# Two weight splits moved behind their chunk's own steps, and the value transposes moved ahead of the chunk loop, with VectorE evicting them

## The reference

```
h = rmsnorm(x, g_mix_pre)
[a | u | v | q | k | vv | gates] = h @ w_in
z = (q . k) * SB_SCALE + bias                       # 8 heads of 64, strictly causal
log_rest = where(mask, log_sigmoid(-z), 0)
after = reverse_cumsum(log_rest) - log_rest         # over the keys behind
C = where(mask, exp(log_sigmoid(z) + after), 0) @ vv
```

## Time and profile before

| | us |
|---|---|
| median of 3 runs | 1888.24 (1886.55 to 1888.35) |
| the profiled execution, its own time | 1886.19 |
| its span | 1884.3 |
| PE busy | 1821.5 (97%) |
| DVE busy | 824.3 (44%) |
| ACT busy | 557.1 (30%) |
| POOL busy | 275.9 (15%) |

### The profile page before, as it was taken

How to read it: one execution, slowest core, us unless ns; L and a number is a source line. 1 busy time by engine, 2 the same in 40 slices (tenths; PEclk the granted TensorE clock), 3 DMA queues, 4 the chain that set the end, 5 groups by cost and what they waited for, 6 DMA issues and landing times.

```text
span 1884.3 us, 28795 instructions
## 1 busy us (share of the span) xinstructions
PE 1821.5 (97%) x11075; PEld 1725.8 (92%) x11075; DVE 824.3 (44%) x1088; ACT 557.1 (30%) x871; POOL 275.9 (15%) x324
## 2 busy tenths in 40 slices
PE   6999999999999999999999999999999999999997
PEld 5778786969699899999999879999999999999996
DVE  5564737374343522233342494442134442344437
ACT  4575748382100100010023452231022220122213
POOL 1121202021143211111101120010000010100013
PEclk9999999999999999999999999999999999999998
DMA  5202030305411111211132031111111111111302
GB/s 164 68 24 67 9 80 0 89 0 149 146 53 49 40 45 39 62 34 50 50 102 90 12 135 45 45 45 45 52 49 45 43 39 51 45 47 52 129 29 95
DMA packets 162280, 113.69 MB, mean 60 GB/s; under 512 B 5389, under 2 KB 152213, under 8 KB 161947
## 3 DMA queue, kind: packets, MB, share of 16 engines
q1 hardware_dynamic: 161035, 108.34, 19.3%
q10 hardware_dynamic: 1200, 4.75, 0.7%
HBM read 95.86 MB, written 13.40 MB: 58 GB/s over the span
## 4 chain that ended last, share of the span: by engine, by line
PE 86%; DVE 5%; ACT 4%; issue 3%; DMA 1%; POOL 0%; SPq 0%; DVEq 0%; ACTq 0%; POOLq 0%
PE ps L1434 66%; PE ps L1444 10%; PE misc L1526 2%; PE misc L1420 1%; PE ps L1700 1%; ACT zl L719 1%; ACT zl L724 1%; PE ps L1510 1%; PE ps L1511 1%; DVE hn L1291 0%; PE ps L1516 0%; DVE trunk L1278 0%; PE ps L1514 0%; DVE h_lo L1295 0%; DMA kv_pg<-in_cache_v 0%
## 5 line engine op out<-in xcount | busy, mean ns | idle before, releaser
L1034 DVE TENSOR_TENSOR w_lo<-stage,w_hi 128x1024 fp32r<-128x1024 f32 x148 | 199.0, 1345 | 593.6 <-POOL w_hi L546 593.1
L1434 PE MATMUL ps<-h_hi,w_lo 128*128 128x344 f32 x1896 | 403.5, 321 | 0.8 <-DVE y_lo L1229 0.8
L1434 PE MATMUL ps<-h_lo,w_hi 128*128 128x344 f32 x1896 | 402.4, 320 | 0.0
L1434 PE MATMUL ps<-h_hi,w_hi 128*128 128x344 f32 x1896 | 400.3, 319 | 0.0
L546 POOL TENSOR_SCALAR w_hi<-stage 128x1024 fp32r<-128x1024 f32 x148 | 157.5, 1065 | 1258.0 <-PE ps L1434 1054.7
L1434 PEld LDWEIGHTS ps<-h_hi,w_lo 128*128 128x128 f32 x1896 | 318.8, 188 | 2.8 <-issue 1.4
L1434 PEld LDWEIGHTS ps<-h_lo,w_hi 128*128 128x128 f32 x1896 | 320.8, 189 | 0.0
L1434 PEld LDWEIGHTS ps<-h_hi,w_hi 128*128 128x128 f32 x1896 | 315.9, 188 | 0.0
L957 ACT ACTIVATE up<-ps 128x1032 f32<-128x1032 f32 x44 | 45.6, 1035 | 354.6 <-PE ps L1434 353.0
L1444 PE MATMUL ps<-h_hi,w_lo 128*128 128x344 f32 x408 | 137.4, 337 | 0.0
L1444 PE MATMUL ps<-h_lo,w_hi 128*128 128x344 f32 x408 | 131.8, 323 | 0.0
(11 more groups left out here) (261 smaller groups left out, 2523.6 us busy)
## 6 DMA issues: line engine op xcount, KB each, us to landing
stage<-in_w_in SPq DMA_DIRECT2D x48, 512.0 KB, 3.9
stage<-in_w_up SPq DMA_DIRECT2D x44, 512.0 KB, 3.8
stage<-in_w_down SPq DMA_DIRECT2D x16, 448.0 KB, 3.3
stage<-in_w_branch SPq DMA_DIRECT2D x24, 256.0 KB, 2.7
x_scratch<-trunk SPq DMA_DIRECT2D x1, 4128.0 KB, 12.6
x_back<-x_scratch SPq DMA_DIRECT2D x1, 4128.0 KB, 12.9
x_tok<-in_x_prompt SPq DMA_DIRECT2D x8, 512.0 KB, 8.1
kv_pg<-in_cache_k SPq DMA_DIRECT2D x16, 256.0 KB, 4.0
```

What stands on the lines that cost most here:

```text
L1034: V.tensor_tensor(w_lo[par][:, :, :], stage[par][:, :, :], w_hi[par][:, :, :].bitcast(F32), ALU.subtract).then_inc(w_lo_made, 1)
L1434: last = M(ps[par][:, c, :], w[par][:, k, :], x[:, c * CH:(c + 1) * CH], start=(k == 0 and s == 0), stop=(k == n - 1 and s == 2))
```

## The change

Three edits, all inside the loop over head pairs.

1. GpSimd issues `split_hi` of steps 7 and 23 behind that step's `s_hi` rather than ahead of it.
2. VectorE issues `split_lo` of the first of them (Q weights) at the end of step 9, behind `sums(9)`, and that of the second (K weights) behind the loop, after `s_lo(23)`.
3. PE transposes the values directly behind the keys, ahead of the scores of chunk 0, into another PSUM tile, `vt_ps`: the first 1024 columns of the second accumulator, which are banks 3 and 4 of the five score banks in turn. VectorE copies them to `v_tok` directly behind the key copy, ahead of the chunk loop. ScalarE no longer has the copy. PE waits for the copy at `VT_FREE`, the first step whose scores go to one of these two banks (step 2), and for the key copy at step 4, where the values product first writes `misc`.

```
--- before.py
+++ after.py
@@ -266,6 +266,8 @@
         in_ps = [misc, ps_flat[1][:, 0:D]]
         z_bank = [banks[(c + (NZ - NCK) % NZ) % NZ] for c in range(NCK)]
         a_bank = banks[NZ]
+        vt_ps = ps_flat[1][:, 0:TP]
+        VT_FREE = min(c for c in range(NCK) if (c + (NZ - NCK) % NZ) % NZ >= NCH)
         HEAD_ROWS = (slice(0, DH), slice(DH, 2 * DH))
 
         def chunks(ap):
@@ -583,14 +585,14 @@
                 for j in range(2):
                     split_hi(j, p * 32 + 32, p * 4 + (2 + j))
                 for c, (hh, kb, q0, W, top, last) in enumerate(CHUNKS):
-                    if c in NEXT_SPLITS:
-                        j = NEXT_SPLITS.index(c)
-                        split_hi(j, p * 32 + 48, p * 4 + (4 + j))
                     pool.wait_ge(sums_made, p * NSUMS + sums_upto[c + 1])
                     pool.wait_ge(cum_ready, p * NCK + (c + 1))
                     pool.sem_inc(hi_begun, 1)
                     nc.gpsimd.tensor_scalar(s_hi[c % 4][:, 0:W], sums[c % 2][:, 0:W], 1.0, 0.0,
                                             ALU.mult, ALU.add).then_inc(hi_ready, 1)
+                    if c in NEXT_SPLITS:
+                        j = NEXT_SPLITS.index(c)
+                        split_hi(j, p * 32 + 48, p * 4 + (4 + j))
             pool.wait_ge(yc_made, NSEG * HP + 1)
             pool.wait_ge(tok_out, 16 * (TOK_DMAS * HP + 1))
             nc.gpsimd.memset(a_raw[:, :, 0:PAD], 0.0).then_inc(pads_made, 1)
@@ -736,11 +738,6 @@
                     A(att[c % 2][:, 0:W], z_bank[c][:, 0:W], ACT.Exp, bias=bias_p[:, hh:hh + 1]
                       ).then_inc(att_ready, 1)
 
-                def value_rows():
-                    act.wait_ge(vtok_ps, p + 1)
-                    act.wait_ge(tok_out, p * (16 * TOK_DMAS) + 16)
-                    A(v_tok[:, :, :].rearrange("p a b -> p (a b)"), misc, ACT.Copy).then_inc(vtok_made, 1)
-
                 def small_rows():
                     act.wait_ge(small_ps, p + 1)
                     A(small_tok.rearrange("p a b -> p (a b)"), a_bank[0:NS, 0:3 * P],
@@ -764,8 +761,6 @@
                         soft_abs(c)
                         soft_exp(c)
                         soft_ln(c)
-                    if c == 0:
-                        value_rows()
                     if c == SMALL_STEP + 1:
                         small_rows()
                 segment_hi(NSEG - 1)
@@ -1078,6 +1073,8 @@
                 dve.wait_ge(ktok_ps, p + 1)
                 dve.wait_ge(tok_out, p * (16 * TOK_DMAS) + 16)
                 V.tensor_copy(k_tok[:, :, :].rearrange("p a b -> p (a b)"), misc).then_inc(ktok_made, 1)
+                dve.wait_ge(vtok_ps, p + 1)
+                V.tensor_copy(v_tok[:, :, :].rearrange("p a b -> p (a b)"), vt_ps).then_inc(vtok_made, 1)
                 dve.wait_ge(biasp_made, p * 2 + 2)
 
                 def sums_lo(c):
@@ -1100,9 +1097,6 @@
                 for c, (hh, kb, q0, W, top, last) in enumerate(CHUNKS):
                     if c - (LAG_VALUES + 2) in SEGMENT_ENDS:
                         segment_lo(SEGMENT_ENDS.index(c - (LAG_VALUES + 2)))
-                    if c in NEXT_SPLITS:
-                        j = NEXT_SPLITS.index(c)
-                        split_lo(j, p * 4 + (4 + j))
                     t = zl[c % 4][:, 0:W]
                     dve.wait_ge(l_ready, p * NCK + (c + 1))
 
@@ -1131,7 +1125,11 @@
                                 "p o t -> p (o t)"), a_bank[:, 0:CH]).then_inc(a_out, 1)
                             if j == NCH - 1:
                                 V.tensor_copy(a_tail[:, :], last_cols(1, PTAIL)).then_inc(tail_cols, 1)
+                    if c - 2 in NEXT_SPLITS:
+                        j = NEXT_SPLITS.index(c - 2)
+                        split_lo(j, p * 4 + (4 + j))
                 sums_lo(NCK - 1)
+                split_lo(1, p * 4 + 5)
                 segment_lo(NSEG - 2)
                 segment_lo(NSEG - 1)
 
@@ -1549,19 +1547,19 @@
                 tokens(misc, k_f).then_inc(ktok_ps, 1)
                 pe.wait_ge(ps_free[0], p * 2 + freed("att", 0, 2))
                 pe.wait_ge(ps_free[1], p + freed("att", 1, 1))
+                tokens(vt_ps, v_f).then_inc(vtok_ps, 1)
                 pe.wait_ge(stack_in, p * 64 + 64)
                 pe.wait_ge(q_pads, 2)
                 for c in range(NCK + LAG_VALUES + 1):
+                    if c == VT_FREE:
+                        pe.wait_ge(vtok_made, p + 1)
                     if c < NCK:
                         scores(c)
                     if 0 <= c - LAG_CUM < NCK:
                         softplus_sums(c - LAG_CUM)
                     pooling_tile(c)
-                    if c == 0:
+                    if c == LAG_VALUES:
                         pe.wait_ge(ktok_made, p + 1)
-                        tokens(misc, v_f).then_inc(vtok_ps, 1)
-                    if c == LAG_VALUES:
-                        pe.wait_ge(vtok_made, p + 1)
                     if 0 <= c - LAG_VALUES < NCK:
                         values(c - LAG_VALUES)
                     if c == SMALL_STEP:
```

More of the change, by code:

```diff
@@ L737, in weights @@
                       ).then_inc(att_ready, 1)
[L739 to L742, removed]
                 def small_rows():
```

## The result

The changed kernel takes 1873.34 us (median of 4 runs, 1871.02 to 1874.25); the kernel before took 1887.39 in 4 runs on the same chip. That is 14 us faster by the medians. The ratio is 0.9918, with a 95% interval of 0.9906 to 0.9931, which is 13.0 to 17.7 us. Forecast were 1873.5 and a range of 1869 to 1881. The profiled execution took 1871.02 us.

A forecast was written before the change was run, and what follows sets the result against it. The chain was taken as 86% PE, so only PE's waits and lower clock could yield time. Values 2.6, first split 7.7 and clock 3.3 sum to 13.6 us; forecast 1873.5, between 1872.6 and 1874.6, range 1869 to 1881.

The forecast's parts named there:

- The values (2.6 us): Steps 0 to 6: transposing values before chunk 0's scores and copying on VectorE saves 0.66 us per pair, 2.6 in all.
- The 0.66 for ScalarE's lead: Steps 1 to 6, ScalarE the bound: without the value copy, chunk 1 starts 0.66 to 0.7 us earlier.
- The split's wait (7.7 us): Before sums(6): PE's 1.81 us wait for s_lo(6), queued behind the first weight split, goes; 7.7 us over four pairs.
- The control: A pair's second head, same chunks without a split: compared over like scores stretches, it puts the stall at 1.97 us.
- the port shared by VectorE and GpSimd: Steps 7 to 9: w_hi delays s_lo(7) to 290.6 from 289.6, w_lo can delay s_hi(9); cost 0, bounds to 4.2 us.
- The second split (0): Step 23: moving the K weights' split behind s_lo(23) is worth 0, as PE has the next pair's Q products there.
- The clock (3.3 us): Second and fourth pairs: lower-clock stretches of 1.67 us go with the long wait; 3.3 us, bounds 0 and 3.3.
- The clock staying: Head pairs: lower-clock stretches hang on something else or come at the remaining small waits; 1878 us, chance 0.12.
- the stall returning: Step 9 or 10: half of the 7.7 us comes back, likely with a clock stretch or two; 1880 us, chance 0.11.
- a value move worth nothing: Chunk 0: zl(0), 0.8 us late, is carried through sums and s_hi, so no gain there; 1876 us, chance 0.06.
- a gain that doesn't reach the end: After the pairs: a later transfer sets the time, leaving 1888 us; chance 0.04.
- The slower case: GpSimd and VectorE block each other at s_lo(7), s_hi(9), zl(10): 3.5 us per pair, 1892 us; chance 0.04.

The follow-up runs named there:

- the one with `w_hi` ahead: The changed kernel, but GpSimd's w_hi of the first split stays ahead of s_hi(7), with w_lo behind step 9: 1872.07 us, ratio 0.9920.

## Why the prediction was right

**The values (2.6 us).** Right, and a little small: 0.85 us per pair, 3.4 in all. The 0.66 for ScalarE's lead is what moving the copy back to ScalarE costs. The step that it left out: the transposes start 0.2 us sooner after the copy of V than the scores did. In the program they no longer stand behind PE's waits for the stacked K and Q rows; that this is the reason was not tested alone.

**The split's wait (7.7 us).** Right in place and cause. The control gave 1.97; the traces have 1.99 for the pair and 1.97 for scores(8) to scores(11). The first pair's wait was 2.05 us long, not 1.8, so that 8.2 us went in all. The step that the prediction spent its doubt on, whether the port shared by VectorE and GpSimd makes s_lo(7) late, came out as worked: 1.46 us where some 1.7 had been forecast, with 0.43 us to spare and not 0.2. The delay of zl(10) had been put too low, 0.33 us against some 0.1, and that of zl(9), 0.93, had not been reckoned; neither cost PE anything. Of the three places tried for `w_lo` (the ends of steps 6, 7 and 9) only the last is free: at step 7 the split costs 1.2 us per pair and at step 6, with `w_hi` at step 5, 0.7. The end of step 8 was not tried.

**The port.** The Trainium skill's rule ("SBUF — State Buffer", section "Who interferes with whom"), by which the second of two such instructions blocks, agrees with every placement in which they met. s_lo beside a `w_hi` that began first took 1.46, 1.26 and 1.44 us where 0.68 is its own time, and s_hi beside a `w_lo` that began first 1.14 where 0.41 is, and 1.35 where 0.62 is. In the changed kernel and in the one with `w_hi` ahead, s_lo ended 0.53 to 0.54 us behind the end of `w_hi`, so most of its 0.68 us ran only then, while `w_hi` kept its 1.06 us. The trace of the changed kernel also has the controls. All 8 s_lo of 512 columns that met a `w_hi` took 1.45 to 1.46 us, and the other 40 took 0.68 to 0.70. zl of 512 columns, which reads one of its two tiles from PSUM, took 0.74 to 0.75 us in the 40 cases in which GpSimd worked beside it and 0.75 in the other 8.

**The second split (0).** Right: alone it changes nothing.

**The clock (3.3 us).** Right for the two profiled executions: both stretches are gone, and 11.6 + 3.3 make up the 15.0 us between the two marks (11.6 is 4 x 2.84 and 0.25 for the first pair's longer wait). As a mean its size is less sure. Three kernels with the long wait were traced, twelve waits of 1.78 to 2.06 us. Five were followed by a stretch at a lower clock: two in the kernel before, one with the values only, two with the second split only. Each cost 1.60 to 1.67 us between scores(8) and scores(11). That is 1.7 stretches per execution and 2.8 us. In the nine traces of kernels without the long wait, 36 pairs whose longest wait is 1.15 us, there is none between the first pair's scores and the end of the fourth.

The granted clocks of all executions give a second estimate. Their mean is 0.9919 in 41 executions of the kernel before and 0.9939 in 45 of the kernels without the long wait. The missing share times the span is 15.4 and 11.4 us, so 4.0 us, with a standard error of 0.7; it takes in stretches outside the pairs. The 3.3 us lie between the two estimates. With the 11.6 us they give 14.4 to 15.6, inside the 13.0 to 17.7 of the measured ratio.

That the median came within 0.2 us of the forecast is luck. The two underestimates above add up to 1.3 us, the four executions of the changed kernel span 3.2, and the same kernel run again has 1871.98.

**The rivals.** The clock staying, the stall returning, a value move worth nothing, and a gain that doesn't reach the end are excluded by the waits, the pair distances and the total. The slower case needed both blocked instructions on PE's path; they are blocked and not on it.

**What stays open.** Why a wait of 1.8 us is followed by a lower clock in one pair and not in the next, in the same trace, was not tried. Length alone does not decide it: all five cases fell in the second or fourth pair, and the longest waits, 2.05 to 2.06 us in the first pair of each of the three traces, were followed by none.

## What to carry to other kernels

When an engine that works in order does a side job for later, ask which instruction stands behind it and when that one is due; the job belongs where the engine has free time and the next thing due is steps away, not merely behind its step's own work. A like stretch of the loop without the job is a control that gives both the gain and the free time before anything is built. Where two copies could go to either of two engines, give them to the one that isn't the bound in those steps, even if its copy is longer (1.23 us against 1.03 here).

## What the runs showed of the hardware

An instruction of GpSimd that reads SBUF and a VectorE instruction with two SBUF inputs ran almost one after the other in both directions: the first kept its time (`w_hi` 1.06 us), and the recorded duration of the second was stretched by the wait (s_lo 1.46 us for 0.68, s_hi 1.14 for 0.41). A long record isn't slow work. A VectorE instruction with one input in PSUM (zl) was not stretched, 0.75 us either way. And a single idle gap of PE of 1.78 to 2.06 us in an otherwise busy stretch was followed, in 5 cases of 12, by a lower granted clock that cost another 1.60 to 1.67 us, so such a wait can cost nearly twice its length.
